# A PEER decoder block: coefficient gathers asked for earlier, some of their scaling moved to GpSimd, and explicit drains taken out of VectorE's row additions

## The reference, cut to what matters

```python
u = eu[it]                                   # it: 128 expert indices of each token
a = gelu(einsum('ckd,cd->ck', u, ht)) * gt   # one activation per expert and token, times its gate
return einsum('ck,ckd->cd', a, ev[it])       # sum over the 128 experts of a token
```

## Time and profile before

| what | value |
| --- | --- |
| median of 3 runs | 1509.58 us (1508.23 to 1511.9) |
| the profiled execution's own time | 1507.09 us |
| its span | 1505.3 us |
| busy: TensorE, VectorE, GpSimd, ScalarE | 98%, 89%, 68%, 51% |
| granted TensorE clock, mean | 0.991 |
| second pass, about | 770 to 1491 us |

### The profile page before, as it was taken

The page is one execution under the profiler, slowest core; times in us unless marked ns, Lnnn a source line. Parts: engine busy times, 40 slices in busy tenths (PEclk is TensorE's granted clock), DMA queues, the critical chain, the costliest instruction groups (busy, mean ns, idle before and its releaser), DMA issues.

```text
span 1505.3 us, 21851 instructions
## 1 busy us (share of the span) xinstructions
PE 1475.2 (98%) x7296; PEld 1234.4 (82%) x7296; DVE 1334.0 (89%) x2235; ACT 762.0 (51%) x1180; POOL 1021.3 (68%) x732
## 2 busy tenths in 40 slices
PE   7999999999999999999999999999999999999997
PEld 5887778888887888888888888888888888888885
DVE  6497666687999999979979999999999999999998
ACT  4644432433545555554554555555555555555553
POOL 6643223333787777778877777777777777777774
PEclk8999999899999999999999999999999999999999
DMA  9335447222676898989979999999999999999995
GB/s 363 103 106 175 154 154 250 87 84 85 190 242 213 266 307 261 310 264 295 319 277 386 395 398 393 396 403 391 400 397 397 394 397 394 394 399 402 393 395 182
DMA packets 219582, 444.58 MB, mean 295 GB/s; under 512 B 22360, under 2 KB 128984, under 8 KB 219232
## 3 DMA queue, kind: packets, MB, share of 16 engines
q1 hardware_dynamic: 174432, 309.04, 57.9%
q0 software_dynamic: 45056, 134.38, 23.3%
HBM read 407.68 MB, written 35.67 MB: 295 GB/s over the span
## 4 chain that ended last, share of the span: by engine, by line
PE 51%; issue 24%; POOL 19%; DVE 2%; DMA 2%; ACT 0%; DVEq 0%; POOLq 0%; SPq 0%; ACTq 0%
POOL wlo L637 18%; PE ps L1834 15%; PE ps L1843 8%; PE ps L1807 8%; PE ps L1810 8%; PE ps L1813 7%; PE ps L1594 1%; PE ps L1759 1%; PE ps L1818 1%; PE ps L1761 1%; PE ps L1760 1%; DMA raw<-w_stream 1%; DVE ps L1068 1%; DMA coef<-gelu_spill,coef_at 0%; DMA gelu_spill<-gout 0%
## 5 line engine op out<-in xcount | busy, mean ns | idle before, releaser
L637 POOL TENSOR_TENSOR wlo<-raw,whi 128x1024 fp32r<-128x1024 f32 x178 | 428.5, 2421 | 292.7 <-ACT whi L716 291.7
L686 POOL DMA_INDIRECT coef<-gelu_spill,coef_at x256 | 322.9, 1261 | 81.7 <-issue 78.0
L680 POOL DMA_INDIRECT rows<-w_stream,row_at x256 | 242.2, 946 | 77.9 <-issue 77.9
L716 ACT ACTIVATE whi<-raw 128x1024 fp32r<-128x1024 f32 x176 | 186.2, 1060 | 144.8 <-PE ps L1761 97.9
L1834 PE MATMUL ps<-acts,whi 128*128 128x512 f32 x1024 | 253.1, 389 | 0.0
L1834 PEld LDWEIGHTS ps<-acts,whi 128*128 128x128 f32 x1024 | 192.1, 188 | 40.5
L1759 PE MATMUL ps<-whi,acts 128*128 128x512 f32 x512 | 200.3, 391 | 2.2 <-ACT gout L888 2.2
L1760 PE MATMUL ps<-wlo,acts 128*128 128x512 f32 x512 | 199.6, 390 | 0.0
L1761 PE MATMUL ps<-whi,acts 128*128 128x512 f32 x512 | 199.2, 389 | 0.0
L1443 DVE SCALAR_TENSOR_TENSOR ps<-rows,coef,ps 128x1024 f32<-128x1024 f32 x126 | 162.4, 1289 | 11.2 <-issue 0.9
L946 ACT ACTIVATE phi<-prod 128x256 fp32r<-128x256 f32 x128 | 53.6, 419 | 230.1 <-DVE prod L1414 230.1
(11 more groups left out here) (250 smaller groups left out, 2584.0 us busy)
## 6 DMA issues: line engine op xcount, KB each, us to landing
raw<-w_stream SPq DMA_DIRECT2D x304, 512.0 KB, 5.4
values_in<-w_stream SPq DMA_DIRECT2D x128, 512.0 KB, 6.9
ada<-w_ada SPq DMA_DIRECT2D x32, 512.0 KB, 4.5
gelu_spill<-gout SPq DMA_DIRECT2D x64, 256.0 KB, 5.0
gate_spill<-gblock SPq DMA_DIRECT2D x8, 2048.0 KB, 10.4
gates<-gate_spill SPq DMA_DIRECT2D x32, 512.0 KB, 8.1
ada<-w_ada SPq DMA_DIRECT2D x32, 256.0 KB, 7.2
rows<-w_stream,row_at POOLq DMA_INDIRECT x256, 6.4
```

The source lines that it names most:

```text
L637: g.tensor_tensor(wlo[:, s, :], raw[:, s, :], whi[:, s, :].bitcast(F32), ALU.subtract)\
L680: g.indirect_dma_start(rows[m % ROWS][:, :], None, w_front.rearrange("c p n -> (c p) n"), bass.IndirectOffsetOnAxis(row_at[:, t * P + n:t ...
L686: g.indirect_dma_start(coef[:, t, n:n + 1], None, gelu_dram.rearrange("t p g (e o) -> (t p g e) o", o=1), bass.IndirectOffsetOnAxis(coef_a ...
```

## The change

GpSimd asks for one more pair of coefs at each of `n` = 6, 10, 14 and 18, so that from 18 on it is five `n` ahead of the rows instead of one. From the eleventh batch (`b` = 10, that is `n` = 20 and 21) on, the multiplication by the gates is an instruction of GpSimd, placed just ahead of `fetch_rows(2b + 2)`, and VectorE waits for its semaphore `coef_scaled`. The drain ahead of the tile 0 additions is replaced by a wait on `row_added` for the addition before the last one; the drain inside VectorE's `scale_coefs` stays for the first ten batches.

```diff
+MORE_COEFS = tuple(range(6, 6 + 4 * 4, 4))
+SCALED_ON_DVE = 10
...
+            def scale_coefs(b):
+                pool.wait_ge(coef_in[b % COEF_RING], 16 * PAIR * COEFS * (b // COEF_RING + 1))
+                some = slice(b * COEFS, (b + 1) * COEFS)
+                g.tensor_tensor(coef[:, :, some], coef[:, :, some], gate_of[:, :, some], ALU.mult).then_inc(coef_scaled, 1)
+
+            def coefs_asked(n):
+                return min(NK, n + 1 + FIRST_COEFS - FIRST_ROWS + sum(m <= n for m in MORE_COEFS))
+
+            pool.wait_ge(gate_of_ready, 1)
             for n in range(FIRST_ROWS, NK):
+                if n % COEFS == 0 and n // COEFS - 1 >= SCALED_ON_DVE:
+                    scale_coefs(n // COEFS - 1)
                 fetch_rows(n)
-                if n + FIRST_COEFS - FIRST_ROWS < NK:
-                    fetch_coefs(n + FIRST_COEFS - FIRST_ROWS)
+                for m in range(coefs_asked(n - 1), coefs_asked(n)):
+                    fetch_coefs(m)
+            scale_coefs(NK // COEFS - 1)
...
             def add_row(n, t):
 
-                if t == 0:
-                    dve.drain()
-                    if n % COEFS == 0:
+                m = n * PAIR + t
+                if n >= 1:
+                    dve.wait_ge(row_added, m - 1)
+                if t == 0 and n % COEFS == 0:
+                    if n // COEFS < SCALED_ON_DVE:
                         scale_coefs(n // COEFS)
-                m = n * PAIR + t
+                    else:
+                        dve.wait_ge(coef_scaled, n // COEFS - SCALED_ON_DVE + 1)
...
-            v.tensor_copy(gate_of[:, :, :].rearrange("p t n -> p (t n)"), fetched[2])
+            v.tensor_copy(gate_of[:, :, :].rearrange("p t n -> p (t n)"), fetched[2]).then_inc(gate_of_ready, 1)
```

More of the change, by code:

```diff
@@ L388, in build @@
         row_added = sem("row_added")
+        coef_scaled = sem("coef_scaled")
+        gate_of_ready = sem("gate_of_ready")
         turned = sem("turned")
```

## The result

The kernel before took 1510.06 us (median of 4 runs, 1508.23 to 1511.90), the changed one 1678.24 (4 runs, 1676.51 to 1679.69): a ratio of 1.1119 [1.1101, 1.1136], 168 us slower. The forecast was 1517.9 with a range from 1508.5 to 1528. The direction was right, the size off by a factor of 20, and the likeliest case was not the one that came: it was rival 2, at three times its worked price.

The account below looks back on a forecast made before the run. TensorE was taken as the bound at 5.654 us per step. A 9.4 us stall less 0.45 at the head and 0.60 at the tail gave +8.3 on 1509.58, so 1517.9 us, range 1508.5 to 1528.

Parts of the forecast that it names:

- the likeliest case: Early coefs stall TensorE by step 22, its pace holds afterwards: 1517.9 us, own range 1513.5 to 1521, chance 0.60.
- rival 2: After n = 22 GpSimd becomes the bound; one more blocked gather per two steps costs +53 us, 1571; chance 0.15.
- The bound before, and the lock: TensorE paces at 5.654 us per step; GpSimd's gathers are tied to VectorE's step, four in each, 1.413 us apiece.
- It becomes idle time there: VectorE's 34 us saved on drains and scaling lie in front of TensorE's unchanged step, so turn into VectorE idle time.
- I expect TensorE's pace to hold: After n = 22, eight gathers and one scaling take 10.2 us, 11.3 in the lock, within two steps' 11.31.
- The lag of the early coefs, 9.4: Eight extra gathers before n = 22 delay GpSimd 11.3 us; TensorE stands still 9.4 in total by step 22.
- The cover of 5.2: Rows' lead over their additions, about 5.2 us beyond a 6.4 landing, can be lost before VectorE waits, from about row 11.
- The scaling's own price: Each GpSimd multiplication of 4 elements takes 0.2 us, between 0.17 and 0.6.
- the lag of GpSimd must be nil at this place: Batch 10's scaling, ahead of `fetch_rows(22)`, is needed by row 20's addition; VectorE waits for whatever lag is left of 11.3 us.
- Head and tail: Gains from drains and scaling leaving VectorE: 0.45 us at one long first step, 0.60 at the last additions.
- Rivals 1 and 3: First: extra gathers absorbed, 1508.5 us, chance 0.20. Third: TensorE's step hides waits for VectorE, 1501 us, chance 0.05.

Follow-up runs that it names:

- e1b: Kernel before with only the drains replaced by waits on `row_added`; VectorE scales all, no early coefs: 1582.80 us, ratio 1.049.
- e6: Changed kernel without the four additional early pairs of coefs (drains out, GpSimd scales): 1678.69 us, ratio 1.114.
- e5b: Kernel before with only the scaling from the eleventh batch on moved to GpSimd; drains kept, no early coefs: 1551.53 us, ratio 1.028.
- e2b: Kernel before with only the four additional early pairs of coef gathers; drains and scaling stay on VectorE: 1521.76 us, ratio 1.0084.
- e3b: Changed kernel with the drains put back and the waits on `row_added` out: 1562.41 us, ratio 1.035.
- e7: Changed kernel plus a one-column VectorE copy behind each row addition, both tiles: 1525.36 us, ratio 1.0105.
- e10: Changed kernel with a one-column copy behind each row addition and without the early coefs: 1518.85 us, ratio 1.0069.
- e11: Kernel before with drains out and a one-column copy behind each row addition; no early coefs, VectorE scales all: 1570.46 us, ratio 1.041.
- e4: Changed kernel with all scaling left on VectorE (drains out, coefs early): 1552.83 us, ratio 1.030.

## Why the prediction was wrong, point by point

- **The bound before, and the lock:** right. TensorE set the pace, and the gathers were held by VectorE's instructions with both inputs in SBUF, 0.90 behind a start of the next. That rule gives, within 0.03 us, the duration of 509 of the 512 gathers in the trace of before. One reading is off by one: row 24 takes the buffers of row 20, so while row 20 is still to be added the buffers allow 23, not 24. Nothing hung on it.
- **"It becomes idle time there", said of what the drain gives back, 0.17 per step:** this is the step that failed. The drain was priced as VectorE's time alone. The trace of before shows what else it was. `make_value_lo` gives way at 1215.35 (1214.21 and its 1.14), the addition starts at 1215.53, and between the two starts a gather:

```profile
1215.42 0.94 POOL L680 DMA_INDIRECT rows<-w_stream,row_at  x1 [0.30 <-issue]
```

It is not held, and the next, at 1216.67, falls 0.05 ahead of `make_prod`. Without the gap the addition and `make_prod` start 0.17 earlier, the latter at about 1216.55, and that gather is 0.12 behind it. The changed kernel has just this: 927.71 is 0.13 behind 927.58, the gather takes 1.11, and the whole chain behind it is shifted. The prediction had this at nothing. It costs 73 us alone (e1b), and 127 on top of the scaling on GpSimd (e6 against e5b). Rival 2 named this fit ("the gather that slipped in 0.05 us before `make_prod`") and gave it 0.15, with the argument that VectorE idles 0.3 us ahead of `make_prod`. That idle time exists only while GpSimd isn't the late one. Once VectorE waits for L708 it runs its whole row of instructions without a gap, and this argument turns round.
- **"I expect TensorE's pace to hold" after n = 22:** wrong in the same way. The sum of 10.2 or 11.3 us for two steps took the lock as the worst a gather can suffer, 1.41. The trace of before had no 2.02 and no 2.69 in it (its longest gather took 1.78); a gather started at each place of VectorE's row should have been worked out with the rule I had: it "waits for that instruction's end and then needs 0.905". Behind `make_value_lo` that is 1.14 + 0.905 = 2.04, as measured. 2.69 is beyond the rule.
- **The price of rival 2,** 53 us for one gather more per pair of steps: mis-sized. 3.08 us per pair were lost, 148 in the stretch, since a held gather makes its successor held: three in a row and not one.
- **The lag of the early coefs, 9.4:** right in kind, wrong in two terms. Alone (e2b) they make long steps at the rows of n = 7 to 23, and VectorE waits 16.9 us for landings. The cover of 5.2 was not there: rows took 8.0 us to land in the median, not 6.4, and VectorE waited from row 7 on, not 11, so the lead of a row over its addition fell only from 11.6 (882.75 to 894.35, row 20 of before) to 8.2 (897.54 to 905.70). And nothing was regained (I took 1.5 off): GpSimd itself came 14.5 later, counted from the third step, to row 24 (920.84 against 905.27), where the sum had a lag of 11.3. The stretch is 11.6 over that of before, where the prediction's terms, with the cover, gave 4 to 8. The largest wait is row 19's, the first behind the last four extra gathers, and not row 20's. With the scaling on GpSimd added (e3b) row 20 is waited for as well, 3.7 us for L708, and yet the stretch is hardly longer than in e2b, 12.8 against 12.2. The clock was left out: after the pause of 4.29 us the granted clock is at 0.58 from 901.50 to 905.00, near the lower of its two levels, 1.2 GHz; the two products of L1824 take 1.22 instead of 0.63, and from that line to the small product are 2.73 us (902.06 to 904.79) where the step before took 1.46 (891.89 to 893.35). That is 1.3 of this step's 5.8. In the changed kernel the stretch is 20.2 over, and 13.7 of it are there without the early coefs (e6).
- **The scaling's own price,** 0.2 us each: right, 0.214. What it does by being waited for was said ("the lag of GpSimd must be nil at this place") but only for batch 10, and not for the 53 behind it.
- **Head and tail:** the tail's additions follow at 1.19 where it was 1.37 (1663.72, 1664.92 and 1666.11 in the changed kernel), as taken. It is worth a few tenths of a microsecond at most: from the last small product to the span's end are 19.15 us before, 19.50 in the changed kernel and 18.78 in e7. At the head nothing was gained, as the step from 788.14 to 794.46 took 6.32 against 6.12 before.
- **Rivals 1 and 3:** not absorbed, and TensorE holds no hidden waits that VectorE's relief would free: where nothing stalls (e7, e10) two steps take 11.31 as before.
- **The page of the Trainium skill:** "SBUF — State Buffer", section "Who interferes with whom", says that such a VectorE instruction contends with a GpSimd one that reads SBUF, and that the order of issue decides who blocks. The traces agree where VectorE is first, with the 2.02 us above as the plainest case. Where the gather is first VectorE is not held: in the trace of before `again_lo` has the same pitch, 1.135 us in the median, in the 120 cases in which a gather runs on for over 0.3 us past its start and in the 6 without. The section's inference that `tensor_tensor` doesn't hold up descriptor generation is not borne out for these gathers: 2.02 behind `make_value_lo`, a tensor_tensor, against 0.95 where nothing holds them.

What was not settled: why a gather 0.01 behind `make_prod` passes two starts of VectorE and ends behind the third (934.71), while one 0.13 behind it (927.71 behind 927.58) is let go at the first. Where the border lies, the traces do show. In all 18 together 239 gathers start less than 0.035 us behind `make_prod`, and 232 of them take over 2.5 us; 744 start from 0.035 to 0.25 behind it, and one does. Behind `make_value_lo` 717 gathers start within 0.035, none takes over 2.5, and 705 take 1.95 to 2.1. Also open are whether another filler length would keep clear in e11, and the first chip. The 33 us of e4 were not followed step by step either.

## What to carry to other kernels

Where two engines hold each other up, the time of an instruction taken out is not its price: ask what started in its gap, and work out where each instruction of the other engine will start without it, with the measured release rule, for every position. If one such engine is made to wait for the other once per period, the phase is set anew each time and a bad one stays for the whole pass; a test is to add a few hundredths of a microsecond of work and see whether the kernel gets faster. If it doesn't, the phase is not ruled out: the same copies opened another trap in e11.

## What the runs showed of the hardware that was not expected

- An indirect gather of 128 offsets holds GpSimd for 0.945 us if it starts clear, 1.1 to 1.4 or 2.02 if it starts under a VectorE instruction with two inputs in SBUF (it ends 0.90 behind that one's successor's start), and 2.69 if it starts less than 0.035 behind `make_prod` (232 of 239 in all traces). VectorE is not held by a gather that is already running (`again_lo` has a pitch of 1.135 us with one and without). Differences of 0.02 to 0.06 us in the start decide among these (930.60 in the changed kernel against 1209.59 in e7).
- 256 copies of one column, each pushing what follows by 0.06 us, make the changed kernel 153 us faster (1525.36 against 1678.24); with VectorE scaling, the same copies save 12 (e11, 1570.46, against e1b, 1582.80).
- One chip ran the kernel before at 1640 us and three variants of it 2 to 4% faster than that, while on the others before took 1509 and each variant was slower.
